# Cache pages on 64 partitions in pairs: loads of 64 x 2560 bytes in place of 128 x 1280 in a latent-attention decoder step

## The reference, cut to what matters

```
q_lat  = einsum('bthn,chn->bthc', q_nope, w_uk)
s_past = (einsum('bthc,bsc->bhts', q_lat, past_ckv) + einsum('bthr,bsr->bhts', q_rope, past_kpe)) * MLA_SCALE
p      = softmax(concatenate([s_past, s_new]))
o_lat  = einsum('bhts,bsc->bthc', p[..., :past_len], past_ckv) + einsum('bhtu,buc->bthc', p[..., past_len:], ckv_new)
```

## Time and profile before

| | |
|---|---|
| median of 3 runs | 1654.98 us (1652.56 to 1658.53) |
| profiled execution | 1655.77 us, its span 1654.0 us |
| TensorE matmul busy | 1575.3 us (95%) |
| DVE, ACT, POOL busy | 823.1, 556.8, 730.3 us |
| TensorE in the chain that ended last | 81% of the span |

### The profile page before, as it was taken

One profiled execution on the slowest core, in us unless ns is written; L12 is line 12 of the kernel. 1 busy time (PEld: TensorE's weight loads), 2 busy tenths in 40 slices (PEclk: granted clock), 3 DMA queues, 4 the chain that ended last, 5 costly groups with the idle time before them and its releaser, 6 DMA issues.

```text
span 1654.0 us, 28059 instructions
## 1 busy us (share of the span) xinstructions
PE 1575.3 (95%) x10778; PEld 1480.4 (90%) x10778; DVE 823.1 (50%) x1458; ACT 556.8 (34%) x1220; POOL 730.3 (44%) x875
## 2 busy tenths in 40 slices
PE   7999999899999999999999888999899999999997
PEld 6999999799999998999998557999799999977896
DVE  5137301676666757575766430005974421179416
ACT  5013101344444444444444320112232221279422
POOL 3332324155545555455545513456523223279620
PEclk9999999999999999999999999999999999999998
DMA  4112232011112121111126986226254322444223
GB/s 190 55 51 98 81 133 92 21 56 65 64 52 68 55 67 61 54 61 55 60 95 200 337 305 267 77 65 230 76 221 163 129 68 93 169 138 136 83 85 145
DMA packets 101454, 186.92 MB, mean 113 GB/s; under 512 B 11106, under 2 KB 65139, under 8 KB 101043
## 3 DMA queue, kind: packets, MB, share of 16 engines
q1 hardware_dynamic: 86676, 139.36, 25.3%
q0 software_dynamic: 8448, 24.65, 4.3%
q10 hardware_dynamic: 6208, 21.26, 3.2%
HBM read 137.42 MB, written 49.89 MB: 113 GB/s over the span
## 4 chain that ended last, share of the span: by engine, by line
PE 81%; DVE 7%; issue 3%; DMA 3%; ACT 2%; POOL 2%; SPq 1%; POOLq 0%; DVEq 0%; ACTq 0%
PE ps L128 26%; PE ps L992 8%; PE ps L2219 7%; PE ps L1059 6%; PE ps L2427 5%; PE ps L1043 4%; PE ps L998 3%; PE ps L1005 2%; PE ps L1023 2%; PE ps L1025 2%; PE ps L1024 2%; PE ps L1026 2%; PE ps L1027 2%; PE ps L2353 2%; DVE b_rot L875 1%
## 5 line engine op out<-in xcount | busy, mean ns | idle before, releaser
L682 POOL TENSOR_SCALAR b_prob<-b_prob,b_share 128x896 f32<-128x896 f32 (+7 forms) x128 | 97.7, 764 | 191.5 <-DVE b_share L908 189.8
L1875 POOL CAST w_hi_d<-w_raw_d 128x1024 fp32r<-128x1024 f32 x38 | 42.3, 1113 | 226.4 <-PE ps L128 110.9
L128 PE MATMUL ps<-a_xh,w_hi_a 128*128 128x344 f32 x552 | 118.7, 323 | 11.5 <-DVE a_xl L398 10.3
L786 ACT ACTIVATE b_pth<-ps 128x512 fp32r<-128x512 f32 (+1 forms) x160 | 86.2, 555 | 98.7 <-PE ps L1043 89.1
L128 PE MATMUL ps<-a_xl,w_hi_a 128*128 128x344 f32 x552 | 117.5, 321 | 0.0
L128 PE MATMUL ps<-a_xh,w_lo_a 128*128 128x344 f32 x552 | 117.0, 320 | 0.0
L778 ACT ACTIVATE b_prob<-ps,b_least 128x896 f32<-128x896 f32 (+7 forms) x128 | 94.8, 743 | 55.8 <-DVE b_least L900 54.8
L913 DVE TENSOR_TENSOR b_ptl<-ps,b_pth 128x512 fp32r<-128x512 f32 (+1 forms) x160 | 99.0, 632 | 24.8 <-ACT b_pth L786 23.7
L900 DVE TENSOR_REDUCE b_least<-ps 128x1 f32<-128x896 f32 (+7 forms) x128 | 96.2, 752 | 29.9 <-PE ps L1029 29.1
L128 PEld LDWEIGHTS ps<-a_xh,w_hi_a 128*128 128x128 f32 x552 | 93.0, 189 | 12.9 <-issue 10.7
L106 POOL CAST w_hi_a<-w_raw_a 128x1024 fp32r<-128x1024 f32 x23 | 25.0, 1086 | 172.5 <-PE ps L128 168.1
(11 more groups left out here) (356 smaller groups left out, 4582.5 us busy)
## 6 DMA issues: line engine op xcount, KB each, us to landing
w_raw_d<-in_w_tiles SPq DMA_DIRECT2D x46, 512.0 KB, 3.6
c_pages<-in_cache_pages SPq DMA_DIRECT2D x80, 160.0 KB, 4.0
w_raw_a<-in_w_tiles SPq DMA_DIRECT2D x23, 512.0 KB, 3.5
gate_scratch<-a_stage ACTq DMA_DIRECT2D x16, 512.0 KB, 2.6
oh_scratch<-b_oh POOLq DMA_DIRECT2D x64, 128.0 KB, 2.1
ol_scratch<-b_ol POOLq DMA_DIRECT2D x64, 128.0 KB, 2.1
xo_h<-oh_scratch SPq DMA_DIRECT2D x16, 512.0 KB, 11.0
xo_l<-ol_scratch SPq DMA_DIRECT2D x16, 512.0 KB, 10.4
```

The lines of the kernel that those rows point to most:

```text
L128: mm = nc.tensor.matmul(ps[:, bank + c, 0:CH], wt, xt[:, k0 + k, c * CH:(c + 1) * CH], start=first and x == 0, stop=last and x == 2)
L682: nc.gpsimd.tensor_scalar(prob[:, n % 4, 0:keys], prob[:, n % 4, 0:keys], share[:, n % 4:n % 4 + 1], 1.0, ALU.mult, ALU.mult).then_inc(nor ...
L786: nc.scalar.activation(pth[:, n % 4, 0:cols], ps[:, 4 + n % 2, 0:cols], ACT.Copy).then_inc(pt_hi, 1)
```

## The change

Two pages share a slot: page `4c + i` goes to the half `i % 2` of the partitions, and to slot `2c + i // 2` of 8. On each of its 64 partitions a page has 640 numbers: the latents of positions p and p + 64, and then row p of the turned rotary key for all 128 positions. Block n of 128 positions, as transposes and `mix` read it, now holds 64 positions each of two pages. The same bytes are loaded by the same number of DMAs, each with 64 pieces of 2560 bytes in place of 128 of 1280. The matmuls have the same shapes and count; those of the rotary part read runs of 128 numbers where they read runs of 64.

```
-    pages = [at(f"c_pages{r}", [P, NPG, QUAD, PGW], first + r * page_bytes) for r in range(ROUNDS)]
+    pages = [at(f"c_pages{r}", [P, NPG // 2, QUAD, 2 * PGW], first + r * page_bytes) for r in range(ROUNDS)]
...
-            eng.dma_start(pages[r][:, 4 * c + i, s, :], a["cache_pages"][ds(page, 1)].rearrange("a p c -> (a p) c")
+            half = slice(i % 2 * (P // 2), (i % 2 + 1) * (P // 2))
+            eng.dma_start(pages[r][half, 2 * c + i // 2, s, :], a["cache_pages"][ds(page, 1)].rearrange("a p c -> (a p) c")
                           ).then_inc(page_in[by_pool][r * CHUNKS + c], 16)
+
+    def latents(r, n, s):
+        return pages[r][:, n // 2, s, n % 2 * KVL:(n % 2 + 1) * KVL]
...
-                                         pages[r][:, 4 * c + k, s, f * P:(f + 1) * P], g.ident[:])
+                                         latents(r, 4 * c + k, s)[:, f * P:(f + 1) * P], g.ident[:])
...
-                        mm = nc.tensor.matmul(ps[rows, bank, :].rearrange("p (k e n) -> p e k n", k=4, e=2)[:, f - 2],
-                                              q_b[:, f, b, :], pages[r][:, 4 * c:4 * c + 4, s, KVL:PGW],
+                        mm = nc.tensor.matmul(ps[rows, bank, :].rearrange("p (j k e n) -> p e j k n", j=2, k=2, e=2)[:, f - 2],
+                                              q_b[:, f, b, :], pages[r][:, 2 * c:2 * c + 2, s, 2 * KVL:2 * PGW].rearrange(
+                                                  "p j (k n) -> p j k n", k=2),
...
-                    mm = nc.tensor.matmul(ps[rows, 7, 0:KVL], pt[:, n, rows], pages[r][:, n, s, 0:KVL],
+                    mm = nc.tensor.matmul(ps[rows, 7, 0:KVL], pt[:, n, rows], latents(r, n, s),
...
-    folded = x["cache_kpe"][0].reshape(-1, 2, PAGE // 2, ROPE).transpose(0, 1, 3, 2).reshape(-1, P, ROPE)
+    latent_pairs = x["cache_ckv"][0].reshape(-1, 2, PAGE // 2, KVL).transpose(0, 2, 1, 3).reshape(-1, PAGE // 2, 2 * KVL)
+    turned_keys = x["cache_kpe"][0].reshape(-1, PAGE, ROPE).transpose(0, 2, 1)
...
-        "cache_pages": np.concatenate([x["cache_ckv"][0], folded], axis=2), "page_table": x["page_table"],
+        "cache_pages": np.concatenate([latent_pairs, turned_keys], axis=2), "page_table": x["page_table"],
```

## The result

The changed kernel takes 1680.95 us, median of 4 runs (1674.65 to 1682.1), beside 1654.32 us before (4 runs on the same chip): a ratio of 1.0141, 95% interval 1.0121 to 1.0160. It is slower, where the forecast was 1653.5 us and no change; the time lies outside the range. It is the time that the rival "half the ports, in full" had given (1680), but that rival's way to it turned out otherwise in part, so its nearness is partly luck.

The account below looks back on a forecast made before the run. TensorE was taken to bound the kernel, so only its idle time could be won: 0.63 + 0.9, about 1.5 us off 1655.77, gives 1654.3; runs' median 0.8 lower, so 1653.5 us. Range 1649 to 1667 us.

Parts of the forecast that it names:

- half the ports, in full: Rival, page loads: 64 partitions load at half rate, 207 GB/s; +25 us, 1680 us; chance 0.15.
- What bounds the kernel, and what a microsecond is worth: TensorE, busy 1575.3 of 1654.0 us; a microsecond won before `mix(0)` is one of the kernel, later on pages nothing.
- Larger pieces: Page loads: pieces of 2560 bytes raise capacity from about 365 to 385 GB/s, 5% above the rate of issue.
- The drained queue: Page queues: with capacity above the rate of issue, landings fall from 4.6 us to 3.3 us.
- the 1.5 us: End of `mix(0)`: TensorE's waits shrink by 0.63 us at 939.57 and 0.9 us at 917.23, about 1.5 us sooner.
- The issue: DMA instructions for pages: POOL's for 64 rows taken as 546 ns, between 273 and 546; no gain added.
- TensorE: Matmuls: counts and shapes stay, rotary matmuls stay at 379 ns though reading longer runs; effect 0.
- Half the partitions: Page loads to 64 partitions: price taken as nothing, from one store, `new_kpe`, at 330 GB/s or more.
- It decides under 300 GB/s: In the full rival: half rate matters once the page rate is under 300 GB/s; above this the issue hides it.
- the partial one: Rival, page loads: both halves partly in flight at once, rate 240 to 310 GB/s; 1660 us; chance 0.15.

Follow-up runs that it names:

- e1: Changed kernel, but one DMA loads two neighbouring pages to all 128 partitions, pieces of 2560 bytes, half the DMAs; 1656.47 us, ratio 1.0011 to the kernel before.
- e3: Changed kernel, but each page goes to every other partition instead of the lower or upper 64; 1662.93 us, ratio 1.0031 to the kernel before.
- e8: Kernel before, with one more register load from the page table for each of SP's items, slowing SP's issue; 1661.62 us, ratio 1.0035.
- e9: Kernel before, with six groups of stores and loads on half, all or alternate partitions added near 248 us; a single run, 1687.28 us.
- e5: Changed kernel, but POOL issues a chunk's pages only once TensorE begins turning the chunk two before; 1673.43 us, ratio 1.0095 to the kernel before.
- e6: Changed kernel, but an item's first two pages go to the lower half, its last two to the upper; 1681.64 us, ratio 1.0145 to the kernel before.
- e2: Changed kernel, but pages cut into pieces of 1280 bytes, two on each of 64 partitions; 1687.79 us, ratio 1.0188 to the kernel before.

## Why the prediction was wrong, point by point

- *What bounds the kernel, and what a microsecond is worth*: right. The loss before `mix(0)`, 24.5 us in the profiled runs or 23.6 without the 0.9 that stood before, arrived at the end whole: 23 us by the ratio. The medians differ by 26.6 and the two spans by 26.3; of the latter some 3 us arise after 1200 us, in the second layer, which the change doesn't touch.
- *Larger pieces*: the capacity came near. 386 GB/s were measured in e1 beside a taken 385, at share 1.01, though e1 also has half the DMAs. The drained queue didn't come: e1's landings have a median of 7.3 us for pairs of pages, and its time is unchanged within its interval, so the 1.5 us were not seen.
- *The issue*: POOL's price stayed (516 against 546 ns, 546 taken). SP's was given no part of its own for 64 rows, only for POOL's: this is the second step that failed. It rose by 135 ns a page, and a slower issue of that size costs 0.3% by itself (e3, e8).
- *TensorE*: right. The rotary matmuls keep their median of 379 ns; the longest, 634, fall between 1005 and 1006 us, at a granted clock of 0.52.
- *Half the partitions*: this is the step that failed first. I took the price as nothing on the strength of one store of 258 KB at the end of its queue. In e9 that queue again ends at 413 GB/s, in its last full us, and seven stores like `new_kpe` in a row run at 200. A short transfer behind full ones didn't show the rate of a series. The view of stretches doesn't say whose bytes it counts, and the working took the last 264 KB to be those of `new_kpe`; whether they were stays open. In its place the runs showed pages at 247 GB/s and not 356, and waits of 19.0 us. Of the 23 us that the change lost, e3, which differs by the half alone, lost 5; the other 18 hang on the half, with POOL's lead and the clock in them.
  The Trainium skill (SBUF — State Buffer, "Door 1: The DMA port swizzle"), set aside for that row, was right: it has 196 GB/s for 64 partitions, and e9 shows 200 to 207 over 3 and 4 us. On two transfers to the two halves ("Can I just issue two DMAs to hit both halves?") the Trainium skill gives +6%; e9 shows 239 beside 207, 15% more, and the measurement decides.
- *The rival "in full"*: time right (1680 against 1680.95), way half right. It took 207 GB/s, and 247 came; it put 12 us before `mix(0)` and the rest on `xo_h`, but nearly all pages had landed by 976 us and nothing more was lost at `xo_h`. It had the rate too low and left out three things: SP's issue (some 5 us in e3 and e8), POOL's running ahead of SP (7.5 us, e5), and TensorE's half clock. Of the last, what stands behind the last wait counts for `mix(0)`: 8 turns and 16 scores in 1.97 + 3.23 us, where 1.09 + 1.92 stand at full clock, 2.2 us. That these errors cancelled to within 1 us is luck, and how the parts add up in the changed kernel isn't shown. "It decides under 300 GB/s" fits: e3 at 321 lost only what a slower issue can account for.
- *The chances*: 0.15 on the full case and 0.15 on the partial one, with a range that cut off the first, gave one store too much weight against a mechanism that had its price worked out.
- *Two slips in the sums, without weight*: POOL's packets took 0.512 x 16 x 13 us / 693 = 154 ns and not 157, and SP's 32 pages, with 31 steps in 25.9 us, make 3.3 us for four and not 3.45.

## What to carry to other kernels

Keep a DMA's SBUF side on all 128 partitions, or at least on partitions spread over the whole of them: 64 neighbouring ones moved 200 to 253 GB/s where 128 moved 356 to 414, and cutting the data in larger pieces doesn't pay for it. Judge a rate by a series of transfers that is issued like the one planned, not by a single one in the shadow of others. Where two queues share full DMA engines, look at the landings of each: the queue whose data are wanted first may be the one that gets less.

## What the runs showed of the hardware that was not expected

- SP's DMA instruction for a page took 333 ns for 128 partitions with one piece each, of 1280 or 2560 bytes; 468 for 64 partitions with one piece, 475 for every other partition, 537 for 64 partitions with two pieces. POOL's took 546, 516, 535 to 549 and 587. For rows of 4128 bytes on 64 partitions SP's took 597 (e9). Why SP pays more for fewer rows stays open.
- With work waiting on both queues at 248 GB/s, POOL got 2.01 MB to SP's 1.21 in 13 us; before, at 363 GB/s, they were even (2.37 and 2.33). The packets were even: POOL and SP moved 585 and 589 in the changed kernel, 574 and 575 in e6, 660 and 700 in e2, where SP got 0.80 MB to POOL's 2.24. So the queue with the smaller packets got the smaller share of the bytes.
- A queue for the lower half and a queue for the upper half, both always in flight, gave 253 GB/s, no more than one order for both.
